# Two stacked transformer-like blocks on one core: the order of split, mixing, pair copy and finished tiles around a Strassen down projection

## The reference

```python
def conv_ffn(x, w_up, conv_w, conv_b, w_down):
    u = causal_depthwise_conv(x @ w_up.astype(x.dtype), conv_w, conv_b)
    g, val = jnp.split(u, [FFN_DIM_2], axis=-1)
    return (jax.nn.gelu(g) * val) @ w_down.astype(x.dtype)

h = h + conv_ffn(rms_norm_2(h, ffn_norm[layer]), ffn_w_up[layer], ...)
```

## Time and profile before

| | us |
|---|---|
| median of 3 runs (2973.47 to 2975.8) | 2973.61 |
| the profiled execution | 2976.03 |
| its span, first to last instruction | 2974.2 |
| TensorE, busy | 2925.9 |
| VectorE, busy | 1571.2 |
| GpSimd, busy | 1426.7 |
| ScalarE, busy | 1343.0 |

### The profile page before, as it was taken

The page is one execution under the profiler, slowest core; times in us unless marked ns, Lnnn a source line. Parts: engine busy times, 40 slices in busy tenths (PEclk is TensorE's granted clock), DMA queues, the critical chain, the costliest instruction groups (busy, mean ns, idle before and its releaser), DMA issues. The chain is left out here.

```text
span 2974.2 us, 40478 instructions
## 1 busy us (share of the span) xinstructions
PE 2925.9 (98%) x14888; PEld 2417.2 (81%) x14888; DVE 1571.2 (53%) x2478; ACT 1343.0 (45%) x2089; POOL 1426.7 (48%) x823
## 2 busy tenths in 40 slices
PE   9999999999999999999999999999999999999998
PEld 7888888888878788888888877778888787878887
DVE  5667434221073676443221266646666778576765
ACT  4556444222263566453223355544343457443443
POOL 4445355444443654454444352544646542454645
PEclk9999999999999999999999999999999999999999
DMA  4222232333322231323323232123222222323222
GB/s 143 73 93 72 86 123 90 98 99 99 106 71 86 86 95 63 112 94 118 99 93 105 86 99 64 57 65 99 87 98 90 88 93 85 100 91 100 88 97 92
DMA packets 77303, 273.76 MB, mean 92 GB/s; under 512 B 8776, under 2 KB 9416, under 8 KB 77152
## 3 DMA queue, kind: packets, MB, share of 16 engines
q1 hardware_dynamic: 74112, 266.05, 27.4%
q10 hardware_dynamic: 3040, 5.64, 0.5%
HBM read 269.55 MB, written 2.10 MB: 91 GB/s over the span
## 5 line engine op out<-in xcount | busy, mean ns | idle before, releaser
L3164 POOL TENSOR_TENSOR WLO<-WRAW,WHI 128x1024 fp32r<-128x1024 f32 x361 | 874.0, 2425 | 1032.8 <-ACT WHI L1673 1029.9
L906 PE MATMUL ps<-HH,WHI 128*128 128x512 f32 x2144 | 842.1, 393 | 2.6 <-POOL WLO L3164 0.9
L908 PE MATMUL ps<-HH,WLO 128*128 128x512 f32 x2144 | 834.7, 389 | 0.0
L907 PE MATMUL ps<-HL,WHI 128*128 128x512 f32 x2144 | 834.5, 389 | 0.0
L1673 ACT ACTIVATE WHI<-WRAW 128x1024 fp32r<-128x1024 f32 x435 | 456.7, 1051 | 174.6 <-DMA WRAW<-wall 174.2
L906 PEld LDWEIGHTS ps<-HH,WHI 128*128 128x128 f32 x2144 | 402.6, 188 | 90.9 <-issue 5.3
L908 PEld LDWEIGHTS ps<-HH,WLO 128*128 128x128 f32 x2144 | 402.5, 188 | 84.7
L907 PEld LDWEIGHTS ps<-HL,WHI 128*128 128x128 f32 x2144 | 402.8, 188 | 81.1
L2405 DVE TENSOR_TENSOR ACC<-ACC,SQ 128x512 f32<-128x512 f32 x78 | 70.6, 905 | 280.6 <-ACT SQ L1966 271.2
L2923 DVE SCALAR_TENSOR_TENSOR ps<-U,COLS,ps 128x512 f32<-128x512 f32 x192 | 145.1, 756 | 85.2 <-ACT ps L2140 81.8
L3269 POOL TENSOR_SCALAR SG<-SG,RS 128x512 f32<-128x512 f32 (+3 forms) x104 | 109.9, 1066 | 140.1 <-DVE RS L2685 140.1
(11 more groups left out here) (459 smaller groups left out, 5796.7 us busy)
## 6 DMA issues: line engine op xcount, KB each, us to landing
WRAW<-wall SPq DMA_DIRECT2D x502, 512.0 KB, 3.4
y<-X ACTq DMA_DIRECT2D x8, 256.0 KB, 2.0
X<-xin SPq DMA_DIRECT2D x3, 512.0 KB, 7.7
DFT<-dft ACTq DMA_DIRECT2D x4, 258.0 KB, 4.2
PT_IN<-pin ACTq DMA_DIRECT2D x2, 512.0 KB, 3.7
DIL<-dil ACTq DMA_DIRECT2D x1, 768.0 KB, 4.2
X<-xin SPq DMA_DIRECT2D x2, 256.0 KB, 4.7
COLS<-cols ACTq DMA_DIRECT2D x1, 290.5 KB, 5.4
```

Source lines behind the costliest of these rows:

```text
L906: pe.matmul(out_, WHI[w_at], x_hi, start=first, stop=False)
L907: pe.matmul(out_, WHI[w_at], x_lo, start=False, stop=False)
L908: return pe.matmul(out_, WLO[w_at], x_hi, start=False, stop=last)
L3164: pool.tensor_tensor(WLO[:, s, :], whole, WHI[:, s, :].bitcast(F32), ALU.subtract).then_inc(wt_lo, 1)
```

## The change

Four edits, none of which adds or takes away an instruction; only orders within the queues of VectorE and ScalarE change.

1. VectorE, `conv_ffn`: after the fourth tile FTL of the product stands ahead of the three mixing operations. This holds in all 24 iterations.
2. ScalarE, `conv_ffn`: where the unit to be split is a paired one (only at the fourth tile of a chunk's last iteration, where it is unit 2 of `down`), the split stands behind the high half FTH. Elsewhere nothing changes.
3. ScalarE, `down`: the split of a paired unit is parted in `split_kept` (WHI) and `split_sums` (XHI), and the copy for an ended pair stands between them. It also stands ahead of the finished tiles now.
4. `finished_at`, ScalarE and VectorE: finished tiles are handled one unit later: tiles 0 and 1 at unit 4 (before at 3), tiles 2 and 3 at unit 5 (before at 4).

```diff
         def finished_at(st, j):
 
-            if not st.last or j < 3:
+            if not st.last or j < 4:
                 return ()
-            return (0, 1) if j == 3 else tiles_done(st, j - 1)
+            return {4: (0, 1), 5: (2, 3)}.get(j, tiles_done(st, j - 1))
...
             def split_paired(n):
-
-                s, e = n % SLOTS, PAIRED[n] % EXTRA
+                split_kept(n)
+                split_sums(n)
+
+            def split_kept(n):
+
+                s = n % SLOTS
                 act.wait_ge(raw[s], 16 * (n // SLOTS + 1))
                 act.activation(WHI[:, s, 0:KEPT], WRAW[:, s, 0:KEPT], ACT.Copy).then_inc(slot_hi, 1)
+
+            def split_sums(n):
+                e = PAIRED[n] % EXTRA
                 act.wait_ge(*sums_ready(n))
                 act.activation(XHI[:, e, :], XRAW[:, e, :], ACT.Copy).then_inc(wt_hi, 1)
...
                         conv_tail(st, j, r, col(f"ffn_conv_w_2{st.l}_2", t), col(f"ffn_conv_b_2{st.l}", t), 3)
-                        split_of(st, j, r)
+                        paired = st.unit(j, r) + AHEAD in PAIRED
+                        if not paired:
+                            split_of(st, j, r)
...
                             act.activation(FTH[:, 4 * r + j // 2, :], SG[:, j, :], ACT.Copy).then_inc(S["operand_hi_ready"], 1)
+                        if paired:
+                            split_of(st, j, r)
...
             def down(st):
                 for j in range(st.units):
-                    split_of(st, j)
-                    for t in finished_at(st, j):
-                        finished(st, t)
+                    n = st.unit(j) + AHEAD
+                    if n in PAIRED:
+                        split_kept(n)
+                    else:
+                        split_of(st, j)
                     p = ended_at(st, j)
                     if p is not None:
                         act.wait_ge(unit_used, st.unit(j) + 1)
                         if p:
                             act.wait_ge(S["pair_step"], st.at("pair_step", PAIR_STEPS * p))
                         act.activation(TM[:, 0, 0:HALF], ps[pair_bank(p, 0)][:, 0:HALF], ACT.Copy).then_inc(S["first_copied"], 1)
+                    if n in PAIRED:
+                        split_sums(n)
+                    for t in finished_at(st, j):
+                        finished(st, t)
...
                             dve.tensor_tensor(SG[:, j, :], conv_ps[j][:, :], SG[:, j - 1, :], ALU.mult).then_inc(S["product_ready"], 1)
+                            remainder(st, (FTH[:, 4 * r + j // 2, :], FTL[:, 4 * r + j // 2, :]), SG[:, j, :], 1 + j // 2, r)
                             if j == 3:
                                 mixed(st, r, halves(SG), (2, 3, 6, 7))
-                            remainder(st, (FTH[:, 4 * r + j // 2, :], FTL[:, 4 * r + j // 2, :]), SG[:, j, :], 1 + j // 2, r)
```

## The result

The changed kernel takes 2952.48 us (median of 4 runs, 2948.84 to 2954.6), beside 2974.7 for the kernel before on the same chips. The ratio is 0.992, with a 95% interval of 0.9908 to 0.9932: faster by 22.2 us, 0.7 to 0.9%. The forecast was 2944.8, with 2939 to 2960 as the range. The profiled execution took 2954.6 us (span 2952.8, before 2974.2).

The account below looks back on a forecast made before the run. TensorE, busy 98%, bounds the kernel; only its idle time or slow clock can be won. Gains 3 x 5.6 + 4.7 + 4.4 + 4.4 = 30.3 us, or 27.3 with GpSimd first; middle 28.8 gives median 2944.8, range 2939 to 2960.

Parts of the forecast that it names:

- Ceiling and opening: Start of each of six down stages: wait for FTL and slow clock cost 7.14 us, 43 us in all; both vanish.
- What is late next: Unit 3 of down: GpSimd's XLO comes late, TensorE waits about 2.5 us; 4.5 of the 7.14 us remain gained.
- Open stages: Four down stages: VectorE's chain to unit 7 leaves 5.6 us gained each, 0.9 less at 2660.
- rival (a): The 2.5 us wait at unit 3 drops the clock: 2959 us if all six fall, 2952 if half; chance 0.20.
- its own sum: Whole kernel: gain 30.3 us with VectorE going first, 27.3 with GpSimd first; the middle, 28.8, was taken.
- The closing stage: Stage at 2372: norm's sum 4.4 us earlier, about 2.7 us idle before it; gain 4.4 us, bounds 3 and 6.
- the chain: VectorE's additions and sums from the mixed low half to unit 7 of an open stage: 21.5 us, ending at 2123.1.
- the 2.04 us: Closing stage at 2372: unit 6's 2.04 us wait for the pair addition behind finished tiles 0 and 1 should be gone.
- Earlier iterations: 18 iterations where nothing waits: mixing ends some 0.65 us later, costed at nothing; uncovered it would be 12 us.
- rival (d): Later mixing delays VectorE in all 24 iterations by 0.65 or 1.7 us, at worst 2986 us; chance 0.05.
- (b): Sums for unit 3 come sooner, its wait shrinks to 1 us: gain up to 34 us, 2940; chance 0.05.
- (c): The opening wait only shrinks, some 8 us gained in all, 2965; chance 0.08 together with lesser gains.

Follow-up runs that it names:

- The run with the cut instructions: Changed kernel with GpSimd's WLO and XLO of each stage's first paired unit cut in four instructions each, same work: 2958.83 us, ratio 0.9938.
- the filler: Changed kernel plus three unread 256-column matmuls of ones on TensorE in the wait before each stage's second paired unit (18 in all): 2945.92 us, ratio 0.9895.
- the variant with no such wait left: Changed kernel with tiles 2 and 3 finished at unit 4 and three unread matmuls before each stage's second paired unit: 2943.44 us, ratio 0.9889.

## Why the prediction was right where it was, and where not

- **Ceiling and opening (7.14 us a stage).** Right: unit 2 starts 10.88 us after the stage's first matmul, as worked out, in all six stages; before it was 17.1 to 18.0.
- **What is late next.** Right in place and size: XLO of unit 3 ends at 2107.96, which is 15.25 us behind the product's start, where the text had 15.2; the wait is 2.56 us where it had 2.5. VectorE did go first, and the mixed low half ends 9.6 us behind the product's start, where the text had 9.5. The Trainium skill ("SBUF — State Buffer", section "SBUF: two separate sides") has the shared pair of ports held for a whole instruction. The run with the cut instructions agrees: the shorter the holder's instruction, the shorter the wait (2.50 us beside one of 2.58, 0.71 beside parts that average 0.74).
- **Open stages.** 5.6 us forecast, 5.6 measured in the one stage with full clock, and 43.80 us in all four once the clock is held by the filler: the sum was right at full clock.
- **The clock, rival (a).** This step failed in the weighing: "near the first, but between" gave it 0.20, and it came true in four of six stages. The measured 2952.5 us lies in this rival's band, outside the forecast's 2940 to 2950. The size was off the other way: 2.65 us a stage in the text, 1.5 in the trace, since the stretch is 3.4 us long and not 5.3. So it is luck that the time equals the 2952 that the text gives for the clock falling in half the stages: the stretches were more and shorter, and the norm, which this rival leaves out, cost the rest. The table has three open stages 1.4 to 1.6 us short of the forecast each, 4.6 us, and the closing one with and without the slow stretch (286.90, with the filler 285.81) adds 1.1: 5.7 us of the 7.4 by which the profiled execution missed its 2947.2 (the median missed by 7.7). The remaining 2.5 at the closing stage are the norm's, below; 0.6 came ahead of the first stage, and the text had taken 1.5 off its own sum.
- **The closing stage.** 4.4 us forecast, 0.8 measured. The norm's sum came 3.95 us earlier, counted from the stage's start (57.41 to 53.46 us), close to the text; it also foresaw an idle time there, and it was 1.6 us instead of 2.7. It priced that at nothing:

```profile
2404.32 0.39 PE L908 MATMUL ps<-HH,WLO 128*128 128x512 f32 x1
2406.32 1.49 PE L942 MATMUL ps<-ONES,ACC 128*128 128x1 f32 x8 [1.62 <-DVE ACC L2422]
2407.67 0.77 PE L906 MATMUL ps<-HH,WHI 128*128 128x512 f32 x1
2408.24 0.63 PE L907 MATMUL ps<-HL,WHI 128*128 128x512 f32 x1
```

  Behind it matmuls start 0.43 us apart (clock 0.51 in the window above), and the way from the sum to the next feed-forward grew from 230.3 to 233.4 us. That is 3.1 us. The slow unit 3 of this stage delays the norm's sum besides: with the filler it comes 52.19 us behind the stage's start, not 53.46, which is 5.2 us earlier than before. The idle time in front of the sum comes with edit 4: without it the wait is 0.47 us, without edit 3 still 1.76, with edit 2 alone 0.26.
- **Edit by edit.** The text gave the opening to edits 1 and 2 together, edit 3 a share of the chain, edit 4 the 2.04 us. The runs say otherwise: edits 1 and 2 are substitutes at the opening (either alone removes the wait of 4.28 us: 2960.8 and 2950.8, 2952.5 with all), and taking back any one of the four changes the median by less than 1 us, which is no difference that can be measured. The error was to work the sum for all edits at once only. That edit 2 starts GpSimd's WLO of unit 2 1.84 us later stands in the text; that this makes 1.6 us of the wait at unit 3 (2.56 with edit 2, 0.98 without), and that mixing would fit into the gap it leaves, does not.
- **Earlier iterations, rival (d).** Cost nothing, as forecast: 87.18 us between open stages. Rivals (b) and (c) did not come either: the wait at unit 3 is 2.56 us and not 1, and none for FTL is left.

## What to carry to other kernels

Price a step that is moved once for each edit alone, not only for all together: two edits that remove the same wait are worth one, and each still brings its own cost. Behind every wait that is left on TensorE ask for the clock too; if the wait can't be removed, a few matmuls that nobody reads, in a free bank, may hold it (6.6 us here for 18 of them). And follow the idle time when a wait inside a stage is removed: edit 4 took away 1.9 us at unit 6, of which 1.0 reached the norm's sum, and 1.15 us more of idle time in front of that sum brought 3.1 us of slow clock.

## What the runs showed of the hardware

The length of a wait alone does not settle in these traces whether the clock falls behind it. A half-clock stretch followed 7 of 7 waits of 4.28 us and more inside the `down` stages, 16 of 24 of 2.55 us and 3 of 4 of 2.33 us. Before the second paired unit it followed 7 of 12 of 1.98 us, 4 of 6 of 2.0 us with the cut instructions, and none of 30 of 1.26 us or less (filler or not). Before the plain unit 6 it followed neither the wait of 2.04 us nor that of 1.88. At the norm, where eight one-column matmuls follow the wait, it came behind all six waits of 1.62 to 3.86 us, and behind none of 0.5 us or less. The stretch comes up to twelve matmuls after the wait, and lasts about 3.4 us behind most of the shorter waits inside the stages and 5.3 us behind most of the long ones. The changed kernel's four runs go with it: 2948.84 us at a mean granted clock of 0.998, 2950.56 at 0.996, 2954.4 and 2954.6 at 0.995; the variant with no such wait left gives 2943.0 to 2943.8.

A VectorE operation with both inputs in SBUF that meets a running GpSimd instruction ends 0.28 us (256 columns), 0.55 (512) or 1.08 (1024) after it, however early it started; mixing and FTL do so in each of six traces gone through. So 0.42 us became 2.50 beside an instruction of 2.58, and 0.71 beside parts that average 0.74. VectorE's reductions for the sums (4.2 us for four) and its additions from PSUM (0.68) kept their time beside the same instructions.
